# Hybrid attention and state-space layer: masks of the transposed probabilities on VectorE, value products by halves of keys and queries

## What is computed

```python
def banded_sink_attention(q, k, v, sinks):      # 16 query heads, 4 key/value heads, HEAD_DIM 64
    nb = S // W                                 # W = WINDOW = 128: 4 blocks of 128 tokens
    kb, vb = band(k), band(v)                   # keys: the previous block and the own block, 256
    scores = einsum('bnqhgd,bnshd->bnhgqs', qb, kb) * HEAD_DIM ** -0.5
    dist = W + qi - si
    valid = (dist >= 0) & (dist < WINDOW) & (kpos >= 0)
    ...
    p = where(valid, exp(scores - m[..., None]), 0.0)
    probs = p / (p.sum(-1) + exp(sink - m))[..., None]
    out = einsum('bnhgqs,bnshd->bnqhgd', probs, vb)
```

## Time and profile before

| what | value |
|---|---|
| time, three runs | 1031.88, 1033.05, 1033.41 us; median 1033.05 |
| profiled execution | 1032.09 us, of which the span is 1030.4 us |
| PE busy | 1020.3 us, 99% |
| DVE busy | 642.4 us, 62% |
| ACT busy | 465.9 us, 45% |
| POOL busy | 93.6 us, 9% |
| granted TensorE clock, mean | 0.998 |

### The profile page before, as it was taken

How to read it: one execution, slowest core, us unless ns; L and a number is a source line. 1 busy time by engine, 2 the same in 40 slices (tenths; PEclk the granted TensorE clock), 3 DMA queues, 4 the chain that set the end, 5 groups by cost and what they waited for, 6 DMA issues and landing times.

```text
span 1030.4 us, 13442 instructions
## 1 busy us (share of the span) xinstructions
PE 1020.3 (99%) x5095; PEld 832.3 (81%) x5095; DVE 642.4 (62%) x897; ACT 465.9 (45%) x834; POOL 93.6 (9%) x128
## 2 busy tenths in 40 slices
PE   9999999999999999999999999999999999999997
PEld 8887777777888888888888888898888888888886
DVE  7637998684476686895754544566766676641332
ACT  6335556455555636765633222444444444331233
POOL 0001111110222120122220100000000000000000
PEclk9999999999999999999999999999999999999999
DMA  7622221224656424555362743223332223232222
GB/s 218 123 85 82 82 69 55 83 82 114 160 122 168 130 84 128 141 128 150 102 211 83 253 156 104 80 83 104 100 119 85 81 84 120 89 129 89 93 71 81
DMA packets 123499, 116.49 MB, mean 113 GB/s; under 512 B 21342, under 2 KB 111782, under 8 KB 123447
## 3 DMA queue, kind: packets, MB, share of 16 engines
q1 hardware_dynamic: 95509, 94.74, 29.9%
q10 hardware_dynamic: 25346, 12.59, 5.3%
q0 software_dynamic: 2592, 8.46, 2.2%
HBM read 109.41 MB, written 6.36 MB: 112 GB/s over the span
## 4 chain that ended last, share of the span: by engine, by line
PE 87%; DVE 9%; ACT 2%; issue 1%; DMA 0%; SPq 0%; DVEq 0%; ACTq 0%
PE banks L1270 27%; PE banks L1271 26%; PE banks L1272 26%; DVE conv_acc L1218 3%; DVE w_lo L871 1%; PE banks L1375 1%; PE banks L1368 1%; ACT probs L622 1%; PE banks L1363 1%; PE banks L1343 1%; PE banks L1351 1%; DVE probs L963 1%; DVE small L949 0%; DVE scores L946 0%; DMA w_raw<-in_w_in 0%
## 5 line engine op out<-in xcount | busy, mean ns | idle before, releaser
L871 DVE TENSOR_TENSOR w_lo<-w_raw,w_hi 128x1024 fp32r<-128x1024 f32 (+1 forms) x166 | 201.4, 1253 | 124.0 <-ACT w_hi L584 122.8
L584 ACT ACTIVATE w_hi<-w_raw 128x1024 fp32r<-128x1024 f32 (+1 forms) x166 | 164.1, 1037 | 108.9 <-PE banks L1272 107.6
L1270 PE MATMUL banks<-xn_hi,w_hi 128*128 128x512 f32 x528 | 211.8, 401 | 0.0
L1271 PE MATMUL banks<-xn_lo,w_hi 128*128 128x512 f32 x528 | 206.1, 390 | 0.0
L1272 PE MATMUL banks<-xn_hi,w_lo 128*128 128x512 f32 x528 | 206.0, 390 | 0.0
L1270 PE MATMUL banks<-hn_hi,w_hi 128*128 128x512 f32 (+1 forms) x376 | 141.3, 376 | 0.0
L1271 PE MATMUL banks<-hn_lo,w_hi 128*128 128x512 f32 (+1 forms) x376 | 141.2, 375 | 0.0
L1272 PE MATMUL banks<-hn_hi,w_lo 128*128 128x512 f32 (+1 forms) x376 | 141.2, 375 | 0.0
L1270 PEld LDWEIGHTS banks<-xn_hi,w_hi 128*128 128x128 f32 x528 | 99.1, 188 | 29.8 <-issue 9.3
L1272 PEld LDWEIGHTS banks<-xn_hi,w_lo 128*128 128x128 f32 x528 | 99.1, 188 | 21.6
L1271 PEld LDWEIGHTS banks<-xn_lo,w_hi 128*128 128x128 f32 x528 | 99.3, 188 | 18.9
(11 more groups left out here) (222 smaller groups left out, 1460.0 us busy)
## 6 DMA issues: line engine op xcount, KB each, us to landing
w_raw<-in_w_in SPq DMA_DIRECT2D x29, 1024.0 KB, 5.4
w_raw<-in_w_up SPq DMA_DIRECT2D x22, 1024.0 KB, 5.0
decay<-acs_scratch ACTq DMA_DIRECT2D x16, 512.0 KB, 6.1
w_raw<-in_w_ssd_o SPq DMA_DIRECT2D x8, 1024.0 KB, 5.3
w_raw<-in_w_down SPq DMA_DIRECT2D x8, 1024.0 KB, 5.0
w_raw<-in_w_in SPq DMA_DIRECT2D x16, 256.0 KB, 4.6
w_raw<-in_w_attn_o SPq DMA_DIRECT2D x16, 256.0 KB, 4.6
decay_off<-acs_scratch ACTq DMA_DIRECT2D x32, 128.0 KB, 3.7
```

The source lines that it names most:

```text
L584: A.activation(whi[:, c % 2, lo_:hi_], raw[:, c % 2, lo_:hi_], ACT.Copy).then_inc(w_rounded, 1)
L871: V.tensor_tensor(wlo[:, c % 2, lo_:hi_], raw[:, c % 2, lo_:hi_], f32(whi[:, c % 2, lo_:hi_]), ALU.subtract).then_inc(w_split, 1)
L1270: T.matmul(out_, w[0], m[0], start=first, stop=False)
L1271: T.matmul(out_, w[0], m[1], start=False, stop=False)
```

## The change

1. ATT_STAGES: ACT's probs_t_out and POOL's probs_t_prev are gone. DVE gets probs_t_masked, which reads the transposed probabilities from bank 6 itself and makes both masked copies (the previous one only where there is a previous block: 12 of 16 steps).
2. The products with v go by halves: 64 keys x 64 queries. Keys 0 to 63 sum into bank 2, keys 64 to 127 into bank 7. Of the eight parts (previous or own block, two key halves, two query halves) six are computed, since late queries see no early key of the previous block, and early queries no late key of their own. In block 0 four parts are computed, one of them all zeros. Each part is two matmuls (the two heads) of 64 rows x 64 columns with 256 columns streamed.
3. The two banks are added: ACT attended_left copies bank 2 to a new tile attended, DVE attended_sum adds bank 7 to it. a_hi (ACT) and a_lo (DVE) come from attended, a third of a unit later than before. Bank 2 is also a bank of the scores, so PE's values now wait for the last reader of the scores there, and the next scores for attended_left.
4. ATT_AT for steps 11 to 14 grows by a quarter of a unit, and the first load_decay lies one ACT slot (a third of a unit) later.

```diff
--- before.py
+++ after.py
@@ -105,9 +105,9 @@
 SLOTS = {"PE": 2, "ACT": 3, "DVE": 3, "POOL": 1}
 ATT_STAGES = (
     ("PE", "scores", 1), ("PE", "probs_t", 5), ("PE", "values", 7), ("ACT", "own_scores", 1),
-    ("ACT", "exponentials", 4), ("ACT", "probs_t_out", 7), ("ACT", "attended_hi", 10),
-    ("DVE", "mask_and_max", 1), ("DVE", "probabilities", 4), ("DVE", "probs_t_own", 7),
-    ("DVE", "attended_lo", 10), ("POOL", "probs_t_prev", 2))
+    ("ACT", "exponentials", 4), ("ACT", "attended_left", 10), ("ACT", "attended_hi", 11),
+    ("DVE", "mask_and_max", 1), ("DVE", "probabilities", 4), ("DVE", "probs_t_masked", 7),
+    ("DVE", "attended_sum", 10), ("DVE", "attended_lo", 11))
 SSD_STAGES = (
     ("PE", "x_and_bc", 1), ("PE", "products", 4), ("ACT", "load_decay", -7),
     ("ACT", "load_start_decay", 4), ("ACT", "bc_out", 1), ("ACT", "start_decay", 5),
@@ -129,12 +129,14 @@
     return 2 * AT[("xs", 6)] - 1 + 1.875 * (n - N_SSD // 2)
 
 
-ATT_AT = (-4.5, -3.25, -2, -0.5, 1, 2.75, 4.5, 6.25, 8, 9.75, 11.5, 12.75, 14, 15.25, 16.5, 18)
+ATT_AT = (-4.5, -3.25, -2, -0.5, 1, 2.75, 4.5, 6.25, 8, 9.75, 11.5, 13, 14.25, 15.5, 16.75, 18)
 for _n in range(N_ATT):
     for _e, _w, _v in ATT_STAGES:
         ride(_e, int((2 * AT[("bc", 0)] + ATT_AT[_n]) * SLOTS[_e]) + _v, _w, _n)
 for _n in range(N_SSD):
     for _e, _w, _v in SSD_STAGES:
+        if _n == 0 and _w == "load_decay":
+            _v = -6
         ride(_e, int(first_unit(_n) * SLOTS[_e]) + _v, _w, _n)
 for _g in range(NG):
     _n = _g * NT + NT - 1
@@ -213,7 +215,7 @@
 
         S = sb("scores", [P, 2, GQ, P], 128)
         Pr = sb("probs", [P, 2, GQ, P], 132)
-        pt = sb("probs_t", [P, GQ, P], 136)
+        att = sb("attended", [P, 2, GQ, HD], 136)
         ptc = sb("probs_t_cur", [P, 2, GQ, P], 138)
         ptp_of = [sb(f"probs_t_prev{i}", [P, GQ, P], o) for i, o in enumerate((142, 203.5))]
 
...
@@ -541,14 +544,7 @@
                         eng.wait_ge(gs_tanh, 2 * i + u + 1)
                         eng.dma_start(gs_d[2 * i + u], cth[:, u, :]).then_inc(gs_sp[u], 16)
                     for n, what in rides_at("POOL", c, u):
-                        if what == "probs_t_prev":
-                            eng.wait_ge(a_pt, n + 1)
-                            if n >= 2:
-                                eng.wait_ge(a_pv, n // 2)
-                            eng.tensor_tensor(ptp_of[n % 2][:, :, :], pt[:, :, :],
-                                              mprevT[:, :].unsqueeze(1).broadcast_to([P, GQ, P]),
-                                              ALU.mult).then_inc(a_ptp, 1)
-                        elif what == "mask_cb":
+                        if what == "mask_cb":
                             eng.wait_ge(d_bcs, n + 1)
                             eng.tensor_tensor(bncb[:, P:2 * P], bncb[:, P:2 * P], tri[:, :],
                                               ALU.mult).then_inc(d_cbm, 1)
@@ -623,20 +619,18 @@
                                          accum_out=rsum[:, n % 2, j:j + 1]).then_inc(a_exp, 1)
                         eng.wait_ge(a_df, n + 1)
                         A.activation(es[:, n % 2, :], es[:, n % 2, :], ACT.Exp).then_inc(a_es, 1)
-                    elif what == "probs_t_out":
-                        eng.wait_ge(a_tp, n + 1)
-                        if n:
-                            eng.wait_ge(a_ptc, n)
-                            eng.wait_ge(a_ptp, n)
-                        A.activation(pt[:, :, :], PS[:, 6, :].rearrange("p (j q) -> p j q", j=GQ),
-                                     ACT.Copy).then_inc(a_pt, 1)
+                    elif what == "attended_left":
+                        if n % 2:
+                            eng.wait_ge(a_pv, n // 2 + 1)
+                            A.activation(att[:, :, :, :].rearrange("p h j q -> p (h j q)"), PS[:, 2, :],
+                                         ACT.Copy).then_inc(a_left, 1)
                     elif what == "attended_hi":
                         if n % 2 == 0:
                             continue
                         g, b = att_step(n)
-                        eng.wait_ge(a_pv, n // 2 + 1)
-                        A.activation(a_hi[:, (g // 2) * GQ:(g // 2) * GQ + GQ, b * P:(b + 1) * P],
-                                     PS[:, 7, :].rearrange("p (j q) -> p j q", j=GQ),
+                        eng.wait_ge(a_sum, n // 2 + 1)
+                        A.activation(a_hi[:, (g // 2) * GQ:(g // 2) * GQ + GQ, b * P:(b + 1) * P]
+                                     .rearrange("p j (h q) -> p h j q", h=2), att[:, :, :, :],
                                      ACT.Copy).then_inc(a_oh, 1)
                     elif what == "load_decay":
                         g, cc = n // NT, n % NT
@@ -962,12 +956,21 @@
                         eng.wait_ge(a_rd, n + 1)
                         V.tensor_tensor(Pr[:, k, :, :], Pr[:, k, :, :], bcast(rden[:, k, :], GQ, P),
                                         ALU.mult).then_inc(a_pr, 1)
-                    elif what == "probs_t_own":
-                        eng.wait_ge(a_pt, n + 1)
+                    elif what == "probs_t_masked":
+                        eng.wait_ge(a_tp, n + 1)
                         if n >= 2:
                             eng.wait_ge(a_pv, n // 2)
-                        V.tensor_tensor(ptc[:, n % 2, :, :], pt[:, :, :], tri[:, :].unsqueeze(1).broadcast_to([P, GQ, P]),
-                                        ALU.mult).then_inc(a_ptc, 1)
+                        pt = PS[:, 6, :].rearrange("p (j q) -> p j q", j=GQ)
+                        if att_step(n)[1]:
+                            V.tensor_tensor(ptp_of[n % 2][:, :, :], pt, mprevT[:, :].unsqueeze(1).broadcast_to([P, GQ, P]),
+                                            ALU.mult)
+                        V.tensor_tensor(ptc[:, n % 2, :, :], pt, tri[:, :].unsqueeze(1).broadcast_to([P, GQ, P]),
+                                        ALU.mult).then_inc(a_ptm, 1)
+                    elif what == "attended_sum":
+                        if n % 2:
+                            eng.wait_ge(a_left, n // 2 + 1)
+                            av = att[:, :, :, :].rearrange("p h j q -> p (h j q)")
+                            V.tensor_tensor(av, av, PS[:, 7, :], ALU.add).then_inc(a_sum, 1)
                     elif what == "attended_lo":
                         if n % 2 == 0:
                             continue
@@ -975,8 +978,9 @@
                         tl = slice((g // 2) * GQ, (g // 2) * GQ + GQ)
                         tok = slice(b_ * P, (b_ + 1) * P)
                         eng.wait_ge(a_oh, n // 2 + 1)
-                        V.tensor_tensor(a_lo[:, tl, tok], PS[:, 7, :].rearrange("p (j q) -> p j q", j=GQ),
-                                        f32(a_hi[:, tl, tok]), ALU.subtract).then_inc(a_ol, 1)
+                        V.tensor_tensor(a_lo[:, tl, tok].rearrange("p j (h q) -> p h j q", h=2), att[:, :, :, :],
+                                        f32(a_hi[:, tl, tok]).rearrange("p j (h q) -> p h j q", h=2),
+                                        ALU.subtract).then_inc(a_ol, 1)
                     elif what == "x_dt":
                         eng.wait_ge(d_x, n + 1)
                         if n:
@@ -1327,22 +1331,40 @@
                                     ins.then_inc(a_sc, 1)
                     if what == "probs_t":
                         eng.wait_ge(a_pr, n + 1)
-                        take(6, a_pt, n + 1)
+                        take(6, a_ptm, n + 1)
                         for j in range(GQ):
                             ins = T.transpose(PS[:, 6, j * P:(j + 1) * P], Pr[:, n % 2, j, :], ident[:, :])
                         ins.then_inc(a_tp, 1)
                     if what == "values" and n % 2:
                         g, b_ = att_step(n - 1)
-                        eng.wait_ge(a_ptc, n + 1)
-                        eng.wait_ge(a_ptp, n + 1)
-                        take(7, a_ol, n // 2 + 1)
-                        for back in (1, 0) if b_ else (0,):
+                        eng.wait_ge(a_ptm, n + 1)
+                        take(2, a_left, n // 2 + 1)
+                        take(7, a_sum, n // 2 + 1)
+
+                        def part(keys, queries, back, start, stop):
+
                             for hh in range(2):
-                                rows = slice(hh * HD, (hh + 1) * HD)
-                                probs = ptp_of[hh][:, :, :] if back else ptc[:, hh, :, :]
-                                ins = T.matmul(PS[rows, 7, :], v[:, b_ - back, (g + hh) * HD:(g + hh + 1) * HD],
-                                               probs.rearrange("p j q -> p (j q)"), start=back == 1 or b_ == 0,
-                                               stop=back == 0)
+                                ks, qs = slice(keys * HD, keys * HD + HD), slice(queries * HD, queries * HD + HD)
+                                probs = ptp_of[hh][ks, :, qs] if back else ptc[ks, hh, :, qs]
```

(19 more changed lines are left out.)

5 lines of the change are left out of this document (3 added, 2 removed).

## The result

| what | before | after |
|---|---|---|
| median of 20 runs each, side by side | 1032.75 us (1031.84 to 1033.41) | 1033.79 us (1032.98 to 1035.51) |
| ratio, 95% interval | | 1.0014 [1.0009, 1.0020]: +1.04 us |
| profiled execution, span | 1032.09, 1030.4 us | 1033.96, 1032.2 us |
| POOL's instructions | 128 | 112 |

The forecast was 1034.1, or +1.06 against the three runs known then (median 1033.05). Measured are 1033.79 and +1.04. The interval leaves zero out: the change costs about 1 us, 0.1%.

A forecast was written before the change was run, and what follows sets the result against it. PE, busy 99%, bounds the kernel, with DVE nearly full from 92 to 183 us. -2.46 + 0.06 - 2.82 + 1.58 + 1.49 + 0.76 + 0.60 + 1.85 = +1.06 us: 1034.1, range 1030.8 to 1037.2.

The forecast's parts named there:

- PE's own work: Products with the values: 0.41 us less for each of six pairs, -2.46; block 0 +0.06 for two pairs.
- The old waits: PE standing behind DVE at transposes of steps 5, 7, 9 and products of steps 8 and 9: 2.82 us, all removed.
- step 5: PE's wait at its transposes, behind DVE's late probabilities, which start at 123.86 in place of 123.10: 1.58 us.
- step 7: PE's wait at its transposes, with DVE 1.46 us behind after masks of steps 5 and 6 and pair 5's sum: 1.49.
- step 15: PE's wait at its transposes, with probabilities starting near 234.1 and not 231.72: 1.85 us.
- unit-27 stand: In unit 27 ACT's a_hi lies behind conv_tanh, so DVE stands 2.9 us at a_lo.
- POOL's interference: POOL's masks slow DVE: 1.1 us of DVE come back in unit 26, about as much near 105, 142 and 235 us.
- The decay load: First decay load goes out at about 245 in place of 242.63; ACT has 3.49 us to give before conv_tanh: no cost.
- DVE over 93%: Sign of being right: DVE busy over 93% from 92 to 183 us (82.1 + 8 - 3.5 of 91).
- (a): Rival: DVE keeps up, new waits at most the old ones: -2.4, 1030.6, down to 1027.8 with none; chance 0.17.
- (b): Rival: round trips compound, ACT's a_hi waiting for DVE's sum from unit 20 on: +1.06 + 2.5, 1036.6; chance 0.25.
- (c): Rival: the products' halves do not overlap on PE, +0.85 us for each of eight pairs: 1039.3; chance 0.03.

The follow-up runs named there:

- e7: Changed kernel without DVE's sum: bank 2 is copied but its share left out, a_hi and a_lo come from bank 7; 1029.44 us, ratio 0.9978.
- e8: Changed kernel with a_hi made by DVE right behind its sum, not by ACT; 1035.50 us, ratio 1.0029 to the kernel before.
- e9: e7 plus a same-sized DVE sum at the same place, result unused, a_hi not waiting for it; 1032.24 us, ratio 1.0003 to the kernel before.
- e1: Kernel before with only the masks moved to DVE; products, spacing and a_hi/a_lo as before; 1030.49 us, ratio 0.9983.
- e3: Changed kernel with the old ATT_AT spacing of steps 11 to 14; 1033.10 us, ratio 1.0007 to the kernel before.
- e11: Masks on DVE, old spacing, products halved by queries without a sum, plus three idle DVE operations ahead of step 5's probabilities; 1033.09 us, 1.0004 to the kernel before.
- e6: Kernel before with products halved by queries, no sum, old masks on DVE and POOL with ACT's copy; 1032.65 us, ratio 1.0009.
- e2: Kernel before with only the changed products, ACT's copy and DVE's sum; masks and spacing as before; 1034.88 us, ratio 1.0024.
- e4: Changed kernel with a_lo a third of a unit later in DVE's queue; 1034.93 us, ratio 1.0026 to the kernel before.

## Why the prediction was right, step by step

- **PE's own work**: -2.46 and +0.06 forecast, -2.46 and +0.04 measured.
- **The old waits** were replaced, as said. **The new ones**, forecast and measured: step 5 1.58 and 1.82, step 7 1.49 and 1.57, step 9 0.76 and 0.63, products of 8 and 9 0.60 and 0.63, step 15 1.85 and 1.73. Sum 6.28 and 6.38. That the totals agree within 0.02 us (+1.06 and +1.04) is in part luck: each wait was allowed 0.5 and was off by 0.03 to 0.24, in both directions, and products and waits as measured give +1.14, not the +1.01 inside.
- **The mechanism** (lateness of DVE's queue, standing included) is shown by e7, e8 and e9, not only by the fit. Of the 0.24 that step 5 was short, 0.05 is known: a_hi out of attended takes 0.63 and not the 0.58 to 0.59 of the earlier trace rows, where its source is a bank. The unit-27 stand was 2.8 (forecast 2.9). The probabilities of step 15 started at 234.52, on the scale of before 233.87 (forecast 234.1).
- **Two sums in it do not come out as written.** At step 5 the terms given (the sum 0.45 earlier than a_lo was, then 0.60, 0.65 and 0.60 more, less 0.29) lead to 124.21 and a wait of 1.93, not to 123.86 and 1.58; measured are 124.02 and 1.82. What it left unsaid is further idle time of DVE that takes up lateness, such as the 0.26 ahead of w_lo for ACT in the kernel before, gone in the changed one. At step 15 probabilities from 234.1 on would by the same reckoning give about 2.0 and not 1.85; measured are 1.73. For steps 7 and 9 the text gives results without all their terms.
- **Operands in PSUM cost DVE no more**: sum 680 ns and masks 681 to 682, against 683 for the mask out of SBUF. Leaving that term out was right.
- **POOL's interference** was charged at 1.1 us near four places. The sign was right; that it weighs more is likely but not isolated: e1 shows the masks part alone, which also takes ACT's copy away, as a gain of 1.8 us, where my own reckoning of that part gave 0.3 to 0.6. The prediction never split its sum by the two halves of the change; that would have shown that they pull in opposite directions.
- **"The respacing gives just these steps half a unit more, so nothing waits on PE"** failed as a reason. e3 shows that nothing waits there without it, and that it costs 0.6 to 0.7 us at step 15, by putting the sum directly ahead of a_lo. The sum held since my count at step 15 was made in the new order.
- **The decay load** went out at 245.73 (245.08 on the scale of before, forecast 245), and nothing came of it:

```profile
245.73 0.41 ACTq L645 DMA_DIRECT2D decay<-acs_scratch  x1
```

```profile
254.01 0.60 ACT L792 ACTIVATE conv_tanh<-banks 128x512 f32<-128x512 f32 x1 [1.95 <-PE banks L1276]
```

  ACT still waits 1.95 us for PE there (3.49).
- **DVE over 93%** from 92 to 183 was wrong: 92%. The stretch holds six of the new masks and four sums, 6.0 us at 0.60 each, and not 8. With 82.10 before and 83.64 now, some 4.5 came back, where 3.5 were forecast. The later start is not the reason: from 92.65 to 183.65 it is 83.61.
- **The rivals**: (a) did not come, the waits are twice the old ones. (b) is there in kind, ACT waits for the sum in 5 of 8 pairs, but what reaches PE is what the sum had charged. (c) did not come. Four of the changed kernel's 20 times lie apart, at 1035.2 to 1035.5. A fall of the clock would put them there, but their mean granted clocks (0.999, 0.999, 0.998, 1.000) are like those of the other sixteen (0.998 to 1.000), unlike in e11; the cause is open.

## What to carry to other kernels

Where a second engine is at 90% beside a full PE, weigh each microsecond saved on PE against what the saving makes that engine do in the same stretch: 2.4 us saved on PE cost 4.2 through eight small sums and their round trips (e7 against the changed kernel, inside). Where a round trip between two engines cannot be avoided, put work between its two ends that needs nothing the other engine has queued behind it (e3 at step 15), not the trip's next instruction. Split a product so that each bank is complete (by queries, not by keys), and nothing has to be added. Measure the halves of a change apart: here one half was worth -1.8 us, and the other took that and 1 us more. And where DVE is short, look whether an elementwise operation of POOL lies beside one of DVE with its inputs in SBUF; here taking such masks off POOL paid before anything else did.

## What the runs showed that I had not expected

- POOL's mask holds a DVE operation on 4 columns for its whole rest (0.16 to 0.88, 0.17 to 1.30 us) and leaves the taps out of a bank alone (2.31 us with it). A shift of some tenths of a us decides which it meets, and that is 1.13 of the 1.54 us by which PE's wait at step 5 grew in e6 (0.42 to 1.96).
- A wait of PE of 1.99 to 2.54 us was followed by up to 8 us at a partly lowered clock, which cost about 1.6 us more (e2, e8, e11). It does not happen each time (e4, e6, and by the times half of e11).
- ACT's rounding of 512 columns takes 632 ns out of SBUF and 590 ns out of a bank (0.58 to 0.59 us in e9 too, with the output laid out as in the change), the other way round from what one might think of a copy kept at hand.
